# A chunked delta-rule recurrence rewritten as a software pipeline over token blocks, with transposed copies kept on the other half of the partitions

## The reference

```python
def _rwkv7_step(S, inp):
    r, w, k, v, kk, b = inp
    sa = jnp.einsum('bhvk,bhk->bhv', S, kk)
    S = S * w[:, :, None, :] - sa[..., None] * b[:, :, None, :] + v[..., None] * k[:, :, None, :]
    return S, jnp.einsum('bhvk,bhk->bhv', S, r)

def _rwkv_bidir(rin, S0_f, S0_b):
    r, decay, kd, v, kk, bd = rin
    S_f, y_f = lax.scan(_rwkv7_step, S0_f, (r, decay[:, :, 0], kd[:, :, 0], v, kk, bd[:, :, 0]))
    S_b, y_b = lax.scan(_rwkv7_step, S0_b, (r, decay[:, :, 1], kd[:, :, 1], v, kk, bd[:, :, 1]),
                        reverse=True)
    return S_f, S_b, y_f + y_b
```

## Time and profile before

| what | value |
|---|---|
| median of 3 runs | 4870.73 us (4864.91 to 4880.74) |
| the profiled execution, first to last instruction | 4866.1 us |
| TensorE busy, its weight loads | 4241.5 us (87%), 3280.6 us |
| VectorE, ScalarE, GpSimd busy | 2749.5, 1537.1, 1475.8 us |
| the recurrence in layer 0 | from 557.8 us to 1039.6 us |
| the recurrence in layer 1 | from about 2119 us to about 2593 us |

### The profile page before, as it was taken

The page is one execution under the profiler, slowest core; times in us unless marked ns, Lnnn a source line. Parts: engine busy times, 40 slices in busy tenths (PEclk is TensorE's granted clock), DMA queues, the critical chain, the costliest instruction groups (busy, mean ns, idle before and its releaser), DMA issues. The chain is left out here.

```text
span 4866.1 us, 103654 instructions
## 1 busy us (share of the span) xinstructions
PE 4241.5 (87%) x43026; PEld 3280.6 (67%) x43026; DVE 2749.5 (57%) x4666; ACT 1537.1 (32%) x2721; POOL 1475.8 (30%) x1090
## 2 busy tenths in 40 slices
PE   6999889877998799989986998689788988978898
PEld 4887688854667587778884666578545677854566
DVE  3465444455666447544445665665575656557565
ACT  1332222223552123222222553210155421015542
POOL 2232233302013323233331111565232135523213
PEclk8999999988999899989998999789899999989999
DMA  6455532342135445642324133533403253340325
GB/s 194 146 186 189 145 78 59 81 159 83 42 83 178 148 153 198 197 122 71 78 59 148 45 92 112 172 99 106 149 7 81 67 183 124 104 142 17 81 53 181
DMA packets 517941, 561.41 MB, mean 115 GB/s; under 512 B 112732, under 2 KB 412284, under 8 KB 515380
## 3 DMA queue, kind: packets, MB, share of 16 engines
q1 hardware_dynamic: 389876, 475.93, 31.6%
q10 hardware_dynamic: 127616, 78.95, 5.6%
HBM read 366.75 MB, written 192.23 MB: 115 GB/s over the span
## 5 line engine op out<-in xcount | busy, mean ns | idle before, releaser
L1096 PE MATMUL pr_acc<-hH,pr_wh 128*128 128x512 f32 (+1 forms) x1288 | 482.4, 375 | 0.0
L1097 PE MATMUL pr_acc<-hL,pr_wh 128*128 128x512 f32 (+1 forms) x1288 | 466.0, 362 | 0.0
L1098 PE MATMUL pr_acc<-hH,pr_wl 128*128 128x512 f32 (+1 forms) x1288 | 465.6, 361 | 0.0
L2586 ACT ACTIVATE an_p<-an_p,an_stat 128x1280 f32<-128x1280 f32 (+5 forms) x372 | 339.7, 914 | 162.8 <-DVE an_stat L2664 157.2
L2033 POOL TENSOR_TENSOR rk_ml<-rk_lmask,rk_g 128x384 f32<-128x384 f32 x240 | 232.1, 999 | 464.1 <-DVE rk_g L1963 464.1
L2526 PE MATMUL an_t<-ident,an_p 128*128 128x128 f32 x2152 | 319.5, 283 | 40.3 <-ACT an_pT L2593 27.8
L2619 POOL TENSOR_TENSOR an_kl<-an_k,an_kh 128x1280 fp32r<-128x1280 f32 (+3 forms) x36 | 78.5, 2179 | 898.5 <-DVE an_qh L2644 898.5
L2526 PEld LDWEIGHTS an_t<-ident,an_p 128*128 128x128 f32 x2152 | 236.7, 142 | 163.9 <-issue 68.0
L2660 DVE CUSTOM_DVE_ANT_0 an_p<-an_s,an_mask 128x256 f32<-128x256 f32 (+8 forms) x308 | 274.9, 892 | 101.7 <-PE an_s L2509 68.4
L1971 DVE TENSOR_TENSOR rk_tu<-rk_tu,rk_ps 128x512 f32<-128x512 f32 x300 | 190.3, 634 | 237.0 <-PE rk_ps L1796 237.0
L1465 POOL TENSOR_TENSOR sp_sl<-sp_w,sp_sh 128x512 fp32r<-128x512 f32 x172 | 246.0, 1437 | 196.8 <-DVE sp_sh L1540 178.4
(11 more groups left out here) (382 smaller groups left out, 10181.1 us busy)
## 6 DMA issues: line engine op xcount, KB each, us to landing
CHK<-ri_out SPq DMA_DIRECT2D x24, 1920.0 KB, 8.1
rk_in<-CHK SPq DMA_DIRECT2D x120, 384.0 KB, 5.9
pr_w<-in_w_in ACTq DMA_DIRECT2D x58, 512.0 KB, 4.1
UT<-pr_out SPq DMA_DIRECT2D x45, 640.0 KB, 4.6
sp_w<-in_w_in ACTq DMA_DIRECT2D x50, 512.0 KB, 5.2
U<-sp_c SPq DMA_DIRECT2D x100, 256.0 KB, 2.0
mod_w<-in_w_mod SPq DMA_DIRECT2D x16, 1024.0 KB, 8.0
mo_w<-in_w_out SPq DMA_DIRECT2D x16, 1024.0 KB, 9.6
```

Of the source, the lines that this page charges most:

```text
L1096: nc.tensor.matmul(out, wh[:, u, k, 0:m], hi, start=(k == 0), stop=False)
L1097: nc.tensor.matmul(out, wh[:, u, k, 0:m], lo, start=False, stop=False)
L1098: ins = nc.tensor.matmul(out, wl[:, u, k, 0:m], hi, start=False, stop=(k == KT - 1))
L2586: nc.scalar.activation(row, row, ACT.Exp, bias=stat[:, n % NPM, j, 1:2], scale=heads[groups[n][0]].scale, accum_out=total[:, n % 4, j:j + ...
```

## The change

The names of the tiles stay. What is different:

1. **Order.** The blocks become a software pipeline. During the levels of block b, TensorE also does the `solve` and `outputs` of block b-1 (levels 1 and 2), its two `state` steps (level 3), and `grams`, `turned`, `start_t` and `bv` of block b+1 (levels 2 to 5). `X`, `V` and `BK` get a second buffer for it, and `MN` loses its second one.
2. **Halves.** The transposed copy of each chunk's inverse now lies on the other half of the partitions: `TU` is indexed by chunk, and chunk `c`'s transpose stands at `half[1 - c]`. One of the two products in `level_d` writes to the other half, `level_w` reads from it, and x = 0 of `grams` (beta times kappa) is written to it.
3. **More and fewer products.** `grams` has 24 products for a pair (16 of 64 columns and 8 of 128, where there were 16 of 128), `start_t` has 16 where it had 8. All others keep their number: a block has 720 instead of 672.
4. **Banks.** `level_d` of all pairs writes to the same two banks (`d_at`: one for each chunk), so each waits for VectorE's subtraction of the one before it.
5. **Other engines.** GpSimd makes the start `U0` first (two operations of 256 columns) and then five instead of six level masks. ScalarE's copy of the start is 512 wide instead of 256. VectorE's subtraction is the same size; at the last level it is two operations on 64 partitions. VectorE keeps the copy of the turned beta rows.
6. **DMAs.** The receptance rows are loaded once more into a tile of their own (`receptances`, two transfers of 192 KB for a block). `load(b + 1)` is issued when `turned` of block b-1 is done, but in SyncE's program order behind `store(b - 2)`. The decays are loaded once at the start; the constants are loaded behind the first block.
7. All engines' programs are written out for ten blocks, without loops.

The core of the diff:

```diff
+        X = core.sb(s, "rk_x", [P, 2, NP, 4, P])
+        V = core.sb(s, "rk_v", [P, 2, NP, 2, P])
+        BK = core.sb(s, "rk_bk", [P, 2, NP, 4, P])
+        MN = core.sb(s, "rk_mn", [P, NP, 4, P])
+        w_bank = bank[2:4]
+        def by_chunk(i):
+            return banks[:, i * 512:(i + 2) * 512].rearrange("p (c k) -> p c k", c=2)[:, :, 0:4 * CH].rearrange("p c (q k) -> p c q k", k=CH)
+        d_at, start_at = by_chunk(4), by_chunk(6)
...
+                for b in range(NB):
+                    if b and b + 1 < NB:
+                        sp.wait_ge(pt.sem, pt.nth(NP * b))
+                        load(b + 1)
+                    receptances(b)
+                    if b:
+                        store(b - 1)
...
-                                    ins = nc.tensor.matmul(o, D[rows, u, g, d, arr, tok], D[rows, u, g, d, A_KT:A_RT + 1, tok],
-                                                           start=True, stop=True)
+                        for x, arr, a0, n in ((0, A_BH, A_KT, 1), (1, A_BH, A_RT, 1), (2, A_KH, A_KT, 2)):
+                            for c, h in tiles:
+                                o = gram_at[g][h][half[1 - c if x == 0 else c], d * 256 + x * CH:d * 256 + (x + n) * CH]
...
 -                def level_w(b, u, lv, g):
+                def level_w(b, lv, g):
-                            ins = nc.tensor.matmul(wbank(u, k)[half[c], q * CH:(q + 1) * CH], ML[half[c], u, g, d, h, lv, :],
-                                                   TU[half[c], u, g, q, 0, :], start=True, stop=True)
+                            far = half[1 - c]
+                            ins = nc.tensor.matmul(w_bank[k % 2][half[c], q * CH:(q + 1) * CH], ML[far, u, g, d, h, lv - 1, :],
+                                                   TU[far, u, g, c, q, :], start=True, stop=True)
...
 -                def level_d(b, u, lv, g):
+                def level_d(b, lv, g):
-                                nc.tensor.matmul(o[half[c], q, 0, :], TU[half[c], u, g, q, 1, :], Ws[half[c], g, q, :],
+                                nc.tensor.matmul(d_at[half[1 - c], c, q, :], TU[half[c], u, g, c, q, :], Ws[half[c], g, q, :],
...
-                            ins = nc.tensor.matmul(o[half[c], q, 1, :], Ws[half[c], g, q, :], TU[half[c], u, g, q, 1, :],
+                            ins = nc.tensor.matmul(d_at[half[c], c, q, :], Ws[half[c], g, q, :], TU[half[c], u, g, c, q, :],
...
+                    level_w(b, 1, 0)
+                    level_w(b, 1, 1)
+                    if before:
+                        solve(b - 1, 0)
+                    level_w(b, 1, 2)
+                    level_d(b, 1, 0)
+                    if before:
+                        solve(b - 1, 1)
+                    level_d(b, 1, 1)
+                    if before:
+                        solve(b - 1, 2)
+                        outputs(b - 1, 0)
+                    level_d(b, 1, 2)
...
+                    level_w(b, 5, 2)
+                    level_d(b, 5, 0)
+                    if more:
+                        start_t(b + 1, 1)
+                        bv(b + 1, 0)
+                    level_d(b, 5, 1)
```

More of the change, by code:

```diff
@@ L1674, in _ @@
                     sp.dma_start(lm[:, d, :, :], T["mask_level"][d]).then_inc(cst.sem, 16)
[L1675 to L1690, removed]
@@ L1705, in _ @@
[L1705 to L1709, removed]
+                sp.dma_start(ec[:], T["EC"].rearrange("g p d c -> p g d c")).then_inc(cst.sem, 16)
+                load(1)
+                for b in range(NB):
[5 more added lines that the diff above has]
+                        store(b - 1)
@@ new lines, in start_t, with bv @@
+                            nc.tensor.matmul(start_at[far, c, q, :], U0[far, g, q, :], pair[far, :], start=True, stop=True)
+                        for c in range(2):
+                            far = half[1 - c]
+                            ins = nc.tensor.matmul(start_at[half[c], c, q, :], pair[far, :], U0[far, g, q, :], start=True, stop=True)
+                    ins.then_inc(pu.sem, 1)
+                def bv(b, g):
+                    u = b % 2
+                    pe.wait_ge(ax.sem, ax.nth(NP * b + NP))
+                    if g == 1:
+                        pe.wait_ge(dbk.sem, dbk.nth(NP * b + NP))
+                    if g == 2:
+                        pe.wait_ge(ab.sem, ab.nth(NP * b + 1))
@@ L1947, in _, with turned, start_t @@
-                each(act, block_of)
+                def turned(b, g):
+                    u, first = b % 2, turned_at[g][0]
+                    act.wait_ge(pt.sem, pt.nth(NP * b + g + 1))
+                    nc.scalar.copy(X[:, u, g, :, 0:HD], first[:, 0:256].rearrange("p (q k) -> p q k", k=HD))
+                    nc.scalar.copy(V[:, u, g, :, :], first[:, 256:512].rearrange("p (d k) -> p d k", k=P)).then_inc(ax.sem, 1)
+                def start_t(b, g):
+                    act.wait_ge(pu.sem, pu.nth(NP * b + g + 1))
+                    nc.scalar.copy(TU[:, b % 2, g], start_at).then_inc(au.sem, 1)
@@ new lines, in _ @@
+                turned(0, 0)
+                turned(0, 1)
+                start_t(0, 0)
+                turned(0, 2)
+                start_t(0, 1)
+                bv(0, 0)
+                bv(0, 1)
+                start_t(0, 2)
+                bv(0, 2)
+                for b in range(NB):
+                    before, more = b > 0, b + 1 < NB
+                    level(b, 1, 0)
+                    level(b, 1, 1)
+                    if before:
+                        solved(b - 1, 0)
+                    level(b, 1, 2)
+                    if before:
+                        solved(b - 1, 1)
+                        solved(b - 1, 2)
+                    for lv in (2, 3, 4):
+                        for g in range(NP):
+                            level(b, lv, g)
+                    if more:
+                        turned(b + 1, 0)
+                        turned(b + 1, 1)
+                    level(b, 5, 0)
+                    level(b, 5, 1)
+                    if more:
+                        start_t(b + 1, 0)
+                        turned(b + 1, 2)
+                    level(b, 5, 2)
+                    if more:
+                        start_t(b + 1, 1)
+                        bv(b + 1, 0)
+                        bv(b + 1, 1)
+                        start_t(b + 1, 2)
+                        bv(b + 1, 2)
@@ new lines, in level @@
+                def level(b, lv, g):
+                    k = number(b, lv, g)
+                    dve.wait_ge(pd.sem, pd.nth(k + 1))
+                    if lv < NL:
+                        o = TU[:, b % 2, g, :, :, :]
+                        nc.vector.tensor_tensor(o, o, d_at, ALU.subtract).then_inc(dl.sem, 1)
+                    else:
+                        for c in range(2):
+                            o = TU[half[c], b % 2, g, c, :, :]
+                            ins = nc.vector.tensor_tensor(o, o, d_at[half[c], c, :, :], ALU.subtract)
+                        ins.then_inc(dl.sem, 1)
```

573 lines of the change are left out of this document (311 added, 262 removed).

## The result

The changed kernel takes 4906.20 us (median of 6 runs, 4890.77 to 4919.43), the kernel before beside it 4873.18 us. The ratio is 1.0064, 95% interval 1.0045 to 1.0083: slower by some 31 us. A second measurement gave 1.0070 (1.0054 to 1.0087). The forecast was no change at 4867. The time lies inside the range, on the side that had a chance of 0.26.

A forecast was written before the change was run, and what follows sets the result against it. TensorE's instruction fetch, 256 a page, was taken to bind. Start 585, pages 408.8, loads 30.2 and smaller terms 13.5 ended a stage at 1037.5 us: 4 us less over both layers, 4867 us, range 4795 to 4915.

The forecast's parts named there:

- The first rival: In the recurrence, instruction fetch doesn't bind and pauses belong to `outputs` alone: 194 us less, 4677 us; chance 0.09.
- The pages: TensorE's code in a block, in fetches of 256 instructions: 10.6 before, 11.3 after; 105.5 and 112.8 in a stage.
- The steady block: A block in the recurrence: 9.3 pages x 3.71 plus 2 under a load x 5.60, 45.6 us against 45.8.
- the receptance rows' 0.6: Extra loading of these rows in each block delays a page that meets it: 0.6 us, a fifth of a load's bytes.
- the accumulator's 0.3: `level_d` waits for VectorE since all pairs share one accumulator: 0.3 us a block left uncovered.
- a quiet page: 256 TensorE instructions fetched while no block inputs load: 3.71 us, between 3.50 and 3.91.
- The ends: Outside steady blocks: same page time, plus 3.5 us for the last block's levels 4 and 5 and 2 for the tail.
- Behind it come 110.2 pages x 3.71: From the first level to the stage's end: 112.8 pages less 2.6, at 3.71 us each, 408.8 us.
- The start: Before the first level: a 2.9 us wait for GpSimd goes, constants may give some back; level at 585, before 587.6.
- The baseline of layer 1: Stage end at 1037.5 us against 1039.6 before, taken as 2 us less in each layer, 4 in all.
- The third rival: Load, receptance rows and store collide in level 3, delaying three pages a block: slower, 4897 with that alone; chance 0.26.
- the forecast's two pages: Each load of a block's inputs makes two pages late, 5.60 us each, 1.89 more than quiet ones.

The follow-up runs named there:

- `two_quadrants`: The changed kernel with `level_d`'s products reordered so each group uses two quadrants in turn, instructions equal: 1.0039 of the kernel before, 14 us faster than the changed kernel.
- `small_load`: The changed kernel with most inputs left unloaded from the third block on, 768 KB a load instead of 2688: 0.9981 of the kernel before, 42 us less than the changed kernel.

## Why the prediction was wrong

- **What binds: right.** TensorE stands at pages of 256 instructions. The change took 5.5 to 6.3 us of busy time out of a block and nothing off its length; `two_quadrants` put 1.9 back at no cost. The first rival, which is also what the Trainium skill says (Runtime: NRT & Kernel Launch, Instruction fetch mechanics: the fetch is mostly hidden), gave 4677 and is 229 us off.
- **The pages: right.** Predicted 11.3 a block, found 79 / 7 = 11.3.
- **The steady block: nearly right.** 45.6 us, with the receptance rows' 0.6 and the accumulator's 0.3 it is 46.5; found 46.9 and 46.8. The accumulator's term was 0.24. How the sum splits into pages and load stays open, and part of the agreement can be luck: the seven blocks of `small_load` take 4.03 and 3.95 us a page with 768 KB of a load in each, and 3.95 and 3.87 without the 0.9 us for receptance rows and accumulator, where the forecast had 3.71 for a quiet page. Pages by themselves took 3.79.
- **The ends: the step that failed.** "Behind it come 110.2 pages x 3.71" used a page with nothing in its way as the mean. From the first level to the stage's end the sum gave 452.5 us; layer 0 took 464.8 and layer 1 took 462.7. With the same terms, window by window in layer 0: the seven steady blocks took 2.6 us more than their 79 pages, the first block's levels 4.8 more (8 packets, one load and an accumulator's wait are 33.8 us, and they took 38.6), the last two blocks 1.8 more each (11 and 9 packets), what follows 2.1 more (3 packets). That is 13.1, less 0.8 for fractions of a page. So the ends, 136.3 of the 464.8 us, have four fifths of it. In layer 1 the steady blocks took 1.5 us more and the ends have the rest of 10.2, but the first block's levels only 1.9 of it. A window's share is uncertain by a part of a page; the sums are not. In the first block's levels no earlier block's `solve`, `outputs` and `state` stand between one `level_d` and the next, so that TensorE waits four times for VectorE's subtraction, 3.6 us in all (4.2 in layer 1), and the granted clock was 0.82 (0.95 in layer 1). In the last block, with no next block's work between, such waits are 6.6 us in each layer, where the forecast had 3.8. How much of the ends' time is these waits, and how much pages that took longer than 3.71, no run separates: at 3.79 a page, 110 pages are 9 us a layer more.
- **The start: failed, with its sign.** "I take 585": the first level came at 591.00, 3.7 us too late beside the stage's later start. In layer 1 it was 3.8. The constants stand behind the first block's inputs, and TensorE idles for 6.79 us; the prediction named this and priced it too low. With the constants first the level came at 585.41.
- **The baseline of layer 1: failed.** The sum gave a stage of 1037.5 - 557.8 = 479.7 us and compared it with 481.8, in both layers. In layer 1 the stage took 473.4, so by its own numbers the forecast was 2 us less in one layer and 6 more in the other: +4 and not -4.

Together: 12.3 + 3.7 in layer 0, 14.0 in layer 1 (493.7 against 479.7) and the baseline's 8 are 38 us between the forecast's -4 and the stages' +34.

The third rival had the sign and 4897, for another reason. It wanted three late pages a block under the load, 5.7 us. A load cost between the 2.6 us that `small_load` gave back and some 3.7 by its bytes, no more than the 3.8 of the forecast's two pages.

## What to carry to other kernels

Where code is written out, count the instructions of the engine that binds, in units of 256, before its busy time: an edit that makes records faster and adds instructions can lose, as this one did. Remove waits that others already cover, and give equal weights one wider product; in the kernel before these two gave 1.4%, where the rewrite cost 0.6%. A page timed in quiet windows is not the mean over a stage: sum each stretch of the old kernel with the same model first, ends included, in every place where the stage runs, and forecast the difference of the two sums.

## What the runs showed of the hardware that I had not expected

- A wait that is already met, as an instruction of its own, held TensorE for 94 ns with two waits in it (24 in a row, in the pause shown), and removing one gave 57 ns on average in the kernel before, 35 in the changed one.
- A page of 256 instructions by itself took 3.79 us on average at a granted clock of 1.00, though its records ran in 2.09.
- Under a load without a break pages took longer by about a third: from pause to pause 29.91 / 6 = 4.99 us at a granted clock of 0.50 and 35.84 / 7 = 5.12 at 0.81, while 283 and 290 GB/s were moved:

```profile
2731.59:2761.50 29.91, 21.54 (x768) 21.02 (x768) 0.00 (x0) 0.00 (x0) 0.00 (x0) 0.50 1.08 283
2766.62:2802.46 35.84, 20.34 (x896) 19.38 (x896) 0.00 (x0) 0.00 (x0) 0.00 (x0) 0.81 1.15 290
```
